# Adding the outputs of a mixture of experts by one-hot products instead of scattered rows, with experts grouped in triples

## The chip, the cores and the metric

The kernel runs on one core of one Trainium2 chip. The metric is the device time of one execution in microseconds. TensorE is called PE in the rows (PEld is its weight load), VectorE is DVE, ScalarE is ACT, GpSimd is POOL and the engine that issues most DMAs is SP. Everything is computed in 32-bit floats.

## The reference, cut to what matters

The reference is one layer of a decoder: two attention branches, then a mixture of experts. 320 tokens (256 of a prompt, 64 of eight samples) go through it. Only the second part is touched by the change:

```python
x = x + g1[:, None, :] * ((m_a * o_a + m_b * o_b) @ lw['w_out'])
h2 = modulate(rms_norm(x, lw['norm_ffn_g']), sh2, sc2)
x = x + g2[:, None, :] * hmoe(h2, lw['w_router_grp'], lw['w_router_exp'], lw['w_expert_in'], lw['w_expert_out'])
...
# in hmoe: each token takes one group of 4, and in it the best two of 8 experts
hid = jnp.einsum('nd,edf->nef', t, w_ein)
a, b = jnp.split(hid, 2, axis=-1)
act = jax.nn.silu(a) * b * combine[..., None].astype(hid.dtype)
return jnp.einsum('nef,efd->nd', act, w_eout)
```

There are 32 experts. Each has 1024 x 512 weights in and 256 x 1024 weights out, which is 3.15 MB. Every token goes to two experts, so there are 640 rows of 1024 values to compute and to add up by token. At the end comes a last RMSNorm over the 320 tokens.

## The kernel before, in words

Ahead of the experts the kernel projects the input (L565, L628, L672), runs both kinds of attention (L747 to L1013), the branch and the output projection (L1022, L1038), and routes on VectorE (L1990 to L2190). POOL fills the DRAM tensor `y_rows` (2 x 320 rows of 4 KB) with zeros early on (L2279), among other writes.

The normed rows are stored to DRAM (`h_rows`). Each expert gets slots in a *pair* of 128 slots. There are 16 pairs. Pairs 0 to 2 hold the fixed experts 0 to 5 with 64 slots each. The other 26 experts are sorted by the number of their rows on the chip, and pair `p` from 3 on takes rank `p - 3` (96 slots) and rank `28 - p` (32 slots). Rows beyond an expert's room would go into extra pairs, which run only if there are any.

What happens for pair `p`, with the engine and the line:

- POOL gathers the 128 rows out of `h_rows` (`gather`, L2348). This waits until the buffer of pair `p - 3` has been turned.
- PE turns them (`turn_rows`, L1117), ACT and DVE copy the result out of PSUM (L1497, L2035).
- PE multiplies with the weights in (`hidden`, L1159: 64 products of 32 slots by 512 columns, in two halves of 32, since the weights come in two halves too).
- ACT applies Silu (L1488), DVE multiplies (L2039), PE turns (`turn_act`, L1175), DVE copies (L2043).
- PE multiplies with the weights out (`pair_output`, L1186: 32 products), ACT and DVE scale the two halves by the routing weight into a row buffer `yeS` (L1508, L2049).
- POOL scatters the rows to `y_rows` (`scatter`, L2355).

PE runs `hidden(p)`, `turn_rows(p + 1)`, `pair_output(p - 1)`, `turn_act(p)` in this order. SP issues the weight loads in the order of use. Three pairs fit into SBUF, so that the weights in of pair `p` are asked for when `hidden(p - 3)` is done (L485), and the weights out when `pair_output(p - 3)` is done (L504):

```python
sp.wait_ge(s_hd, p - 2)
...
sp.wait_ge(s_od, 2 * (p - 2))
```

The rows of the last two pairs, 14 and 15, are not scattered. For these the kernel builds a one-hot matrix of 128 slots by 320 tokens on DVE (L2197), and PE multiplies a chunk of 128 channels of the row buffer with it (`early_hits`, L1143; L1245 in the tail): that gives the rows by token and turned. DVE then adds it, gated, to the residual `xT`, in three instructions for each of 8 chunks (`residual`, L1951, L1952, L1954).

The tail comes last: POOL waits for all scatters and signals (L2385), SP loads `y_rows` back in 12 pieces (L542), DVE adds the two rows of each token (L2233), PE turns them (L1240) and adds the product for pair 15 (L1245), DVE adds to the residual, ACT squares (L1544), PE sums (L1248), DVE takes the root's reciprocal (L1573) and scales (L2251), and SP stores the output (L546).

## Time and profile before

| What | Value |
|---|---|
| Median of 3 runs | 753.32 us (751.76 to 755.59) |
| The profiled execution | 755.45 us |
| Its span in the profile | 753.8 us |
| PE busy | 696.9 us (92% of the span) |
| DVE, ACT, POOL busy | 278.3, 172.0, 84.5 us |
| Bytes moved by DMA | 236.15 MB, mean 313 GB/s |
| Weights in, first pair of the sorted experts asked for | at 508 us |

A row of the timeline gives the start, the duration, the engine, the line and the operation with output and input, how many instructions it merges, and in brackets how long the engine had been idle before it and what ended that. The page divides the span into 40 equal slices; each is 18.8 us. "DMA arena<-in_w_ein" as the end of a wait means that a load of weights in landed.

### The profile page before, as it was taken

The page shows a single profiled execution, that of the slowest core. Times are in us where ns is not written, and L with a number is a line of the kernel's source. Part 1 is how long each engine was busy: PE and PEld are TensorE (multiplying, and loading weights), DVE is VectorE, ACT ScalarE, POOL GpSimd, SP SyncE. Part 2 cuts the span into 40 slices and gives each one's busy share as a digit, 9 for nine tenths or more (in the row PEclk, how much of TensorE's full clock was granted, in tenths as well). Part 3 has the DMA queues.
Part 4 walks back from the last instruction along what each step waited for, and adds up shares of the span by engine and source line. Part 5 has one row for each costly group of instructions (what it writes and reads, how often), then busy time and mean ns, then how long its engine had stood idle before and what let it go on. Part 6 is the DMA issues. An engine that isn't in the chain of part 4 may idle for free.

```text
span 753.8 us, 13479 instructions
## 1 busy us (share of the span) xinstructions
PE 696.9 (92%) x5136; PEld 398.8 (53%) x5136; DVE 278.3 (37%) x886; ACT 172.0 (23%) x410; POOL 84.5 (11%) x127
## 2 busy tenths in 40 slices
PE   5899899999999999799998999999999997888894
PEld 2687577558776665454555776664333332222342
DVE  2553123610102787664530322485411211111256
ACT  0223344112102564322242001331110101010102
POOL 0201000002500343110000000001212121112000
PEclk9999999999999999999999999999999999999998
DMA  8999997717344963899999992438999999999981
GB/s 239 383 411 396 410 366 236 309 68 276 113 157 180 359 256 120 313 363 389 392 378 385 420 407 87 191 104 312 419 418 418 418 419 417 419 419 418 420 254 72
DMA packets 63273, 236.15 MB, mean 313 GB/s; under 512 B 9733, under 2 KB 20878, under 8 KB 48293
## 3 DMA queue, kind: packets, MB, share of 16 engines
q1 hardware_dynamic: 52884, 218.73, 74.9%
q0 software_dynamic: 6432, 14.74, 5.3%
q10 hardware_dynamic: 3888, 1.77, 0.9%
q8 instruction: 43, 0.70, 0.4%
q14 instruction: 26, 0.20, 0.1%
HBM read 230.52 MB, written 19.14 MB: 331 GB/s over the span
## 4 chain that ended last, share of the span: by engine, by line
PE 62%; DMA 16%; SPq 13%; DVE 4%; issue 3%; ACTq 1%; ACT 1%; POOL 0%; POOLq 0%; DVEq 0%
PE bank L628 12%; SPq L485 7%; PE bank L1159 5%; PE bank L1038 5%; PE bank L1022 5%; SPq L504 4%; DMA arena<-in_w_eout 4%; DMA arena<-in_w_in 4%; PE bank L672 3%; PE bank L747 2%; PE bank L1186 2%; PE bank L565 2%; PE bank L970 2%; DMA arena<-h_rows,rows_of_slots_in 2%; PE bank L884 2%
## 5 line engine op out<-in xcount | busy, mean ns | idle before, releaser
L1159 PE MATMUL bank<-arena 128*32 128x512 f32 (+1 forms) x896 | 110.9, 610 | 14.2 <-DMA arena<-in_w_ein 14.0
L628 PE MATMUL bank<-arena 128*128 128x320 f32 x384 | 107.6, 439 | 2.8 <-DMA arena<-in_w_in 2.8
L628 PEld LDWEIGHTS bank<-arena 128*128 128x128 f32 x384 | 72.9, 191 | 34.7 <-DMA arena<-in_w_in 3.1
L1159 PEld LDWEIGHTS bank<-arena 128*32 128x32 f32 (+1 forms) x896 | 31.2, 114 | 82.9 <-issue 77.6
L1186 PE MATMUL bank<-arena 128*32 128x512 f32 (+1 forms) x464 | 58.3, 595 | 4.5 <-DMA arena<-in_w_eout 4.1
L2035 DVE COPY arena<-bank 128x512 f32<-128x512 f32 x14 | 9.7, 692 | 108.0 <-PE bank L1117 108.0
L1488 ACT ACTIVATE arena<-bank 128x256 f32<-128x256 f32 x16 | 6.2, 386 | 149.9 <-PE bank L1159 146.9
L1312 ACT ACTIVATE arena<-bank 32x320 f32<-32x320 f32 x60 | 25.8, 430 | 45.5 <-PE bank L628 45.0
L1038 PE MATMUL bank<-arena 128*128 128x320 f32 x128 | 35.0, 432 | 0.0
L1022 PE MATMUL bank<-arena 128*128 128x320 f32 x128 | 34.8, 432 | 0.0
L1186 PEld LDWEIGHTS bank<-arena 128*32 128x32 f32 (+1 forms) x464 | 15.6, 112 | 36.2 <-issue 29.8
L2355 POOL DMA_INDIRECT y_rows<-arena,rows_of_slots_out x14 | 14.1, 1010 | 151.0 <-DVE arena L2049 135.9
L1038 PEld LDWEIGHTS bank<-arena 128*128 128x128 f32 x128 | 24.1, 189 | 10.2
L1022 PEld LDWEIGHTS bank<-arena 128*128 128x128 f32 x128 | 24.1, 189 | 10.3
L1672 DVE TENSOR_TENSOR arena<-arena 128x320 f32<-128x320 f32 x15 | 7.4, 493 | 54.7 <-ACT arena L1313 54.7
L2049 DVE TENSOR_SCALAR arena<-bank,arena 128x512 f32<-128x512 f32 x15 | 11.3, 751 | 44.1 <-PE bank L1186 44.1
L565 PE MATMUL bank<-arena 128*32 128x128 f32 x768 | 23.7, 273 | 0.2 <-DMA arena<-in_w_ada 0.2
L565 PEld LDWEIGHTS bank<-arena 128*32 128x32 f32 x768 | 20.6, 108 | 4.5 <-issue 4.2
L1951 DVE SCALAR_TENSOR_TENSOR arena<-bank,arena 128x256 f32<-128x256 f32 x24 | 11.6, 483 | 28.0 <-PE bank L1038 24.2
L1357 ACT ACTIVATE arena<-arena 128x128 f32<-128x128 f32 (+1 forms) x48 | 21.1, 444 | 2.6 <-DVE arena L1746 2.6
L672 PE MATMUL bank<-arena 128*128 128x512 f32 (+1 forms) x64 | 21.6, 496 | 0.0
L580 PE MATMUL bank<-arena 128*128 128x256 f32 x64 | 16.5, 411 | 4.5 <-DMA arena<-in_cmp_pages 4.5
(413 smaller groups left out, 1011.5 us busy)
## 6 DMA issues: line engine op xcount, KB each, us to landing
arena<-in_w_ein SPq DMA_DIRECT2D x52, 1024.0 KB, 25.2
arena<-in_w_eout SPq DMA_DIRECT2D x26, 1024.0 KB, 26.9
arena<-in_w_ada SPq DMA_DIRECT2D x12, 2048.0 KB, 14.3
arena<-in_w_in SPq DMA_DIRECT2D x10, 2048.0 KB, 10.4
arena<-in_k_pages SPq DMA_DIRECT2D x64, 320.0 KB, 6.0
arena<-in_v_pages SPq DMA_DIRECT2D x64, 320.0 KB, 9.2
arena<-in_w_ein SPq DMA_DIRECT2D x3, 4096.0 KB, 21.8
arena<-in_w_eout SPq DMA_DIRECT2D x3, 2048.0 KB, 13.1
```

Of the source, the lines that this page charges most:

```text
L485: sp.dma_start(wi2[p % 3][:, u, 4 * part:4 * part + 4].rearrange("p k n -> p (k n)"), w_ein[bass.ds(of[u], 1), :, 2048 * part:2048 * part ...
L504: sp.dma_start(wo2[p % 3][:, u].rearrange("p k n -> p (k n)"), w_eout[bass.ds(of[u], 1), :, :].rearrange("o p n -> (o p) n")).then_inc(s_w ...
L565: m = mm(banks[6 + n % 2][32 * j:32 * (j + 1), 0:P].rearrange("p (c d) -> p c d", d=32), condS[:, k, :], columns[:, j], start=(k == 0), st ...
L580: m = mm(banks[2 * v][:, 0:256].rearrange("p (g j m) -> p g j m", g=2, m=4), w1s[v][:, t, :], odd, start=(t == 0), stop=(t == 7))
L628: m = mm(banks[c % 4][:, 0:N], ring[q][:, k, P * (c % 4):P * (c % 4 + 1)], hT[:, k, :], start=(k == 0), stop=(k == KD - 1))
L672: m = mm(bank[0:tn, 0:width], hT[:, k, t0:t0 + tn], ring[q][:, k, 0:width], start=(k == 0), stop=(k == KD - 1))
L1022: m = mm(banks[2 * (c % 2) + a][:, 0:N], wbr_sb[:, 4 * a + k, P * c:P * (c + 1)], src[:, k, :], start=(k == 0), stop=(k == 3))
L1038: m = mm(banks[4 + c % 2][:, 0:N], wo_sb[:, k, P * c:P * (c + 1)], mT[:, k, :], start=(k == 0), stop=(k == KD - 1))
L1159: m = mm(banks[2 + p % 2][r:r + n, :], xeT[p % 2][:, k, r:r + n], wi2[p % 3][:, e, k, :], start=(k == 0), stop=(k == KD - 1))
L1186: m = mm(banks[6 + half][r:r + n, :], actT[:, p % 2, j, r:r + n], wo2[p % 3][:, e, j, 512 * half:512 * (half + 1)], start=(j == 0), stop=( ...
L1312: act(qr[32 * r:32 * (r + 1), c % 3, :], banks[c % 4][32 * (r ^ 1):32 * (r ^ 1) + 32, 0:N], ACT.Copy)
L1357: m = act(seg, seg, ACT.Exp, bias=st[:, 4 + j:5 + j], scale=SCALE, accum_out=st[:, 8 + j:9 + j])
```

## The change

The rows of a unit of work are no longer scattered to DRAM. The kernel multiplies each unit's row buffer with a one-hot matrix, as it did for the last two pairs, and DVE adds the result to the residual chunk by chunk. `y_rows`, its zeros, the scatters, the loads at the end, the sums and the turning in the tail are gone.

There are 12 *units* in place of 16 pairs: the three fixed pairs, one sorted pair (ranks 0 and 25; 96 and 32 slots), and eight triples. Unit `p` from 4 on takes the ranks `p - 3` (64 slots), `p + 5` and `28 - p` (32 slots each). SBUF still holds six experts. Even units use places 2, 3, 4 and odd units 5, 0, 1, so that a triple's weights are asked for when the unit two before it has used that place.

The one-hot products come in halves of four chunks, `by_token(q, half)`. Three tables lay down where PE and DVE do them for an earlier unit `q` while working on unit `p`: before `hidden(p)`, between its halves, and behind it. PE now computes `hidden(p)`, `turn_act(p)`, `turn_rows(p + 1)` and the output of unit `p` itself, in that order, where before the output was that of pair `p - 1`. PSUM banks 0, 1, 3 and 5 take the products, so `hidden` uses bank 2 alone, `turn_act` bank 4 alone, and `turn_rows` waits until two residual chunks have freed banks 0 and 1. The one-hot matrix of a unit is one DVE instruction (`hits_of`). For the last unit the weights out are loaded in two halves by column.

```diff
+UNITS = 12
+LAST = UNITS - 1
+MIDDLE, LIGHT = 9, 17
+BEFORE = {4: (0, 0), 5: (1, 0), 6: (2, 0), 7: (3, 1), 8: (5, 0), 9: (6, 1), 10: (8, 0), 11: (9, 1)}
+AMID = {6: (2, 1), 7: (4, 0), 8: (5, 1), 9: (7, 0), 10: (8, 1), 11: (10, 0)}
+BEHIND = {4: (0, 1), 5: (1, 1), 6: (3, 0), 7: (4, 1), 8: (6, 0), 9: (7, 1), 10: (9, 0), 11: (10, 1)}
...
+            def places_of(p):
+                if p < 4 or p >= UNITS:
+                    return (0, 1) if p >= 3 else (2 * p, 2 * p + 1)
+                return (5, 0, 1) if p % 2 else (2, 3, 4)
...
@@ sync
+            sp.wait_ge(s_hd, 2)
+            unit_in(4, fourth, (0, 1))
+            sp.wait_ge(s_od, 2)
+            unit_out(3, third, (0, 1))
+            sp.wait_ge(s_hd, 3)
+            unit_in(4, fourth, (2,))
+            unit_in(5, fifth, (0,))
...
+            for p in range(6, UNITS):
+                of = experts_of(p)
+                sp.wait_ge(s_hd, p - 1)
+                unit_in(p, of, (0, 1, 2))
+                sp.wait_ge(s_od, 2 * (p - 1))
+                if p < LAST:
+                    unit_out(p, of, (0, 1, 2))
...
-            sp.wait_ge(s_ya, 1)
-            for half in range(2):
-                part = slice(512 * half, 512 * (half + 1))
-                for t, (t0, tn) in enumerate(TOK):
-                    for r in range(2):
-                        sp.dma_start(yR[0:tn, t, r, part], y_rows[N * r + t0:N * r + t0 + tn, part])\
-                            .then_inc(s_yl[3 * half + t], 16)
@@ tensor
+            def by_token(p, half):
+                te.wait_ge(s_hm, p + 1)
+                te.wait_ge(s_yD if half else s_yA, p + 1)
+                for c in range(4 * half, 4 * half + 4):
+                    if 8 * p + c >= 4:
+                        te.wait_ge(s_x2, 8 * p + c - 3)
+                    mm(four_banks[c % 4][:, 0:N], yeS[p % 4][:, P * c:P * (c + 1)], hits[p % 2], start=True, stop=True).then_inc(s_yt, 1)
...
+            for p in range(4, LAST):
+                hidden(p)
+                turn_act(p)
+                turn_rows(p + 1)
+                for half in range(2):
+                    unit_output(p, half)
...
+            with te.If(n_extra < 1):
+                unit_output(LAST, 0)
+                last_by_token(0)
+                unit_output(LAST, 1)
+                last_by_token(1)
+                square_sums()
@@ vector
+            for p in range(4, UNITS):
+                by_token(*BEFORE[p])
+                if p in AMID:
+                    by_token(*AMID[p])
+                pair_act(p)
+                if p < LAST:
+                    by_token(*BEHIND[p], 0, 2)
+                    act_out(p)
+                    by_token(*BEHIND[p], 2, 4)
+                    rows_out(p + 1)
+                    pair_out(p)
+                else:
+                    act_out(p)
+                    by_token(*BEHIND[p])
@@ gpsimd
-            po.dma_start(y_rows.rearrange("(t p) d -> p t d", p=P),
-                         zeros.unsqueeze(1).to_broadcast([P, 2 * N // P, D])).then_inc(s_zf, 16)
...
-            def scatter(p):
-                po.wait_ge(s_yA, p + 1)
-                po.wait_ge(s_yD, p + 1)
-                po.indirect_dma_start(out=y_rows, out_offset=bass.IndirectOffsetOnAxis(row_out[:, p:p + 1], 0),
```

The weights out are stored on the host by column half first. The arithmetic on VectorE that gives each row its slot is changed to fit the units; it has as many steps as before, within a few.

## Rows read from the trace of the kernel before

**Rows 1.** The page, 40 equal slices: bytes moved by DMA in each.
```profile
GB/s 239 383 411 396 410 366 236 309 68 276 113 157 180 359 256 120 313 363 389 392 378 385 420 407 87 191 104 312 419 418 418 418 419 417 419 419 418 420 254 72
```

**Rows 2.** Busy time by stretch: PE, PEld, DVE, ACT, POOL, PEclk, DMA share, GB/s.
```profile
80.00:85.00 5.00, 4.00 (x9) 2.60 (x10) 0.38 (x2) 0.00 (x0) 0.00 (x0) 0.66 1.03 407
508.00:528.00 20.00, 18.94 (x110) 9.50 (x111) 10.27 (x41) 3.24 (x7) 3.32 (x4) 1.00 0.82 303
528.00:718.00 190.00, 171.12 (x1388) 57.02 (x1388) 38.06 (x99) 23.06 (x41) 28.01 (x29) 0.98 1.02 418
718.00:734.00 16.00, 14.58 (x105) 6.28 (x98) 7.34 (x19) 1.76 (x3) 0.00 (x0) 1.00 0.84 249
```

**Rows 3.** Timeline of PE, one pair at full pace, then a wait: start, us, instruction.
```profile
602.36 7.07 PE L1159 MATMUL bank<-arena 128*32 128x512 f32 x64
609.37 1.09 PE L1117 MATMUL bank<-arena 128*128 128x128 f32 x8
610.39 3.64 PE L1186 MATMUL bank<-arena 128*32 128x512 f32 x32
613.96 0.44 PE L1175 MATMUL bank<-arena 128*128 128x128 f32 x2
...
619.17 3.64 PE L1159 MATMUL bank<-arena 128*32 128x512 f32 x32 [1.20 <-DMA arena<-in_w_ein]
```

**Rows 4.** The page, DMA issues: weights of the sorted experts, time from issue to landing.
```profile
arena<-in_w_ein SPq DMA_DIRECT2D x52, 1024.0 KB, 25.2
arena<-in_w_eout SPq DMA_DIRECT2D x26, 1024.0 KB, 26.9
```

**Rows 5.** DMA queues between 528 and 718 us: packets, MB, share of 16 engines.
```profile
q1 hardware_dynamic: 10265, 74.77, 94.5%
q0 software_dynamic: 3888, 4.52, 6.7%
```

**Rows 6.** Timeline of PE and POOL around the early wait.
```profile
59.30 0.90 POOL L2279 DMA_DIRECT2D y_rows<-arena  x1 [0.15 <-issue]
...
76.19 1.98 PE L565 MATMUL bank<-arena 128*32 128x128 f32 x64
81.00 19.23 PE L628 MATMUL bank<-arena 128*128 128x320 f32 x64 [2.83 <-DMA arena<-in_w_in]
...
102.06 17.54 PE L628 MATMUL bank<-arena 128*128 128x320 f32 x64
```

**Rows 7.** DMA between 54 and 81 us: POOL's queue, and two of its issues.
```profile
q0 software_dynamic: 347, 5.09, 48.5%
...
out_win_new<-in_win_state POOLq DMA_DIRECT2D x2, 2016.0 KB, 15.6
y_rows<-arena POOLq DMA_DIRECT2D x1, 2560.0 KB, 29.0
```

**Rows 8.** Timeline of the last two pairs and of the end: start, us, instruction.
```profile
709.65 3.64 PE L1186 MATMUL bank<-arena 128*32 128x512 f32 x32 [0.94 <-DMA arena<-in_w_eout]
713.22 2.42 PE L1143 MATMUL bank<-arena 128*128 128x320 f32 x8
...
714.06 0.48 DVE L1951 SCALAR_TENSOR_TENSOR arena<-bank,arena 128x256 f32<-128x256 f32 x1
...
715.05 0.48 DVE L1951 SCALAR_TENSOR_TENSOR arena<-bank,arena 128x256 f32<-128x256 f32 x1
...
724.66 0.39 ACT L1488 ACTIVATE arena<-bank 128x256 f32<-128x256 f32 x1 [12.33 <-PE bank L1159]
...
726.03 0.42 DVE L2043 COPY arena<-bank 128x256 f32<-128x256 f32 x1 [0.53 <-PE bank L1175]
...
742.51 0.23 DVE L1954 TENSOR_TENSOR arena<-arena 128x64 f32<-128x64 f32 x1
```

**Rows 9.** Timeline of PE: the same 32 products behind two waits.
```profile
651.68 5.22 PE L1159 MATMUL bank<-arena 128*32 128x512 f32 x32 [2.26 <-DMA arena<-in_w_ein]
...
683.76 3.64 PE L1159 MATMUL bank<-arena 128*32 128x512 f32 x32 [1.42 <-DMA arena<-in_w_ein]
```

More of the change, by code:

```diff
@@ L482, in _, with experts_of, half_in @@
                 sp.dma_start(h_rows[RT * t:RT * (t + 1), :], hR[t][0:RT, :]).then_inc(s_hst, 16)
-            def half_in(p, part, of, s):
-                for u in range(2):
-                    sp.dma_start(wi2[p % 3][:, u, 4 * part:4 * part + 4].rearrange("p k n -> p (k n)"),
+            def experts_of(p):
+                ranks = (0, FREE_E - 1) if p == 3 else (p - 3, p + 5, 28 - p)
+                return [sp.value_load(order[0:1, r:r + 1], min_val=0, max_val=E - 1) for r in ranks]
+            def half_in(p, of, part, which):
+                s = s_wh[p % 3] if part else s_wi[p % 3]
+                for u in which:
+                    sp.dma_start(in_of(places_of(p)[u])[:, 4 * part:4 * part + 4].rearrange("p k n -> p (k n)"),
@@ L507, in _ @@
             sp.wait_ge(s_ord, 1)
-            this = sorted_pair(3)
-            after = sorted_pair(4)
-            sorted_in(3, this)
-            for p in range(3, LAST - 1):
-                sorted_in(p + 1, after)
-                sorted_out(p, this)
-                this, after = after, sorted_pair(p + 2)
-            sorted_out(LAST - 1, this)
-            sorted_in(LAST, after)
-            sorted_out(LAST, after)
+            third = experts_of(3)
+            sp.wait_ge(s_hh, 2)
+            half_in(3, third, 0, (0, 1))
@@ L1199, in _ @@
             turn_rows(1, (1,))
-            for p in range(1, LAST):
+            for p in range(1, 4):
                 hidden(p)
@@ L1246, in tail, with square_sums @@
+            def square_sums():
                 for k in range(KD):
@@ L1515, in _ @@
             rows_out(0)
-            for p in range(LAST):
+            for p in range(4):
                 if p:
@@ L1525, in _ @@
                     pair_out(p - 1)
-            pair_out(LAST - 1)
+            pair_out(3)
+            for p in range(4, LAST):
+                pair_silu(p)
+                rows_out(p + 1)
+                pair_out(p)
             pair_silu(LAST)
@@ L1946, in _, with residual @@
             ve.wait_ge(s_x, 32)
-            def residual(c, bank, g0, s, before=0):
+            def residual(c, bank, g0, s, before=0, gated=None):
                 if before + c:
@@ L2222, in extra_pair @@
                 pair_out(p)
+                for c in range(KD):
+                    ve.wait_ge(s_yx, 8 * x + c + 1)
+                    residual(c, banks[5], 40, s_xr, 8 * x, s_xg)
+                ve.wait_ge(s_xr, 8 * (x + 1))
                 if x + 1 < EXTRA // 2:
@@ L2227, in tail @@
             def tail():
-                def row_sums(half, t):
-                    tn, part = TOK[t][1], slice(512 * half, 512 * (half + 1))
-                    ve.wait_ge(s_yl[3 * half + t], yl_before[3 * half + t] + 32)
-                    ve.tensor_tensor(yR[0:tn, t, 0, part], yR[0:tn, t, 0, part], yR[0:tn, t, 1, part], ALU.add).then_inc(s_ysum, 1)
-                def last_residual(first, last):
-                    for c in range(first, last):
-                        ve.wait_ge(s_yt, KD + c + 1)
-                        residual(c, banks[c], 40, s_x2, KD)
-                for t in range(3):
-                    row_sums(0, t)
-                row_sums(1, 0)
-                row_sums(1, 1)
-                last_residual(0, 1)
-                row_sums(1, 2)
-                last_residual(1, KD)
+                for c in range(KD):
+                    ve.wait_ge(s_yt, 8 * LAST + c + 1)
+                    residual(c, banks[LAST_BANKS[c]], 40, s_x2, 8 * LAST)
                 ve.wait_ge(s_ss3, 1)
@@ L2365, in _ @@
             po.wait_ge(s_rows, 3)
-            for p in range(LAST - 1):
-                if p + 3 < PAIRS:
-                    gather(p + 3)
-                scatter(p)
+            for p in range(3, UNITS):
+                gather(p)
             po.wait_ge(s_ord, 2)
@@ L2382, in _ @@
             extra_pair(0)
-            for k in range(3):
-                po.wait_ge(s_ys[k], 16 * ((LAST + 1 - k) // 3))
-            po.memset(cst[:, C_SIN:C_SIN + 1], 0.0).then_inc(s_ya, 1)
 def cond_rows():
```

403 lines of the change are left out of this document (217 added, 186 removed).

## The prediction

> **What bounds the kernel now.** I read the page first and the expert stage after it. The slices of the page show where DMA is full: from the 29th on, ten slices in a row move 417 to 420 GB/s [rows 1]. The windows say the same: 418 GB/s and every DMA engine busy from 528 to 718 us, with PE busy 171 of these 190 us [rows 2]. Which of the two sets the pace shows in the timeline of PE. One pair at full pace takes 7.07 + 1.09 + 3.64 + 0.44, about 12.0 us from one `hidden` to the next [rows 3]. Up to 614 us PE runs at this pace and lives on what was loaded ahead. Then it waits for weights in each pair. An expert is 3.15 MB, so a pair is 6.3 MB, or 15.0 us at 418 GB/s. DMA is the slower of the two. The stage ends when the stream of 26 sorted experts (81.8 MB) ends, plus a tail. The loads of weights take 25 to 27 us to land because they stand in line [rows 4].
>
> When does that stream end? Between 718 and 734 us 16 x 249 GB/s = 4.0 MB arrive [rows 2], and 2.62 MB of them are the 640 rows of 4 KB read back. So 1.36 MB of weights were still to come at 718 us; without the read-back they would be in at 718 + 3.3 = **721.3 us**. From there to 753.8 us is a tail of 32 us, of which the trip through DRAM (last scatter, signal, read-back) takes the most.
>
> I work in times of the profiled execution (755.45 us, span 753.8) and carry the difference over to the median, 753.3 us.
>
> **The scatters.** They go, and with them the bytes in the full stream. By the reference's routing, counted on its inputs drawn with seed 0, pairs 3 to 15 hold 510 rows (gathered after 528 us) and pairs 0 to 13 hold 590 (scattered). Together that is 1100 x 4 KB = 4.51 MB; the trace has 4.52 MB on POOL's queue [rows 5], so the count fits. The scatters' part is 590/1100. By bytes: 2.42 MB / 418 GB/s = 5.8 us. By the queue's share of the engines: 6.7% of 190 us = 12.7 us, times 590/1100 = 6.8 us. I take 6.3 us between them. It counts in full, since the stream is full. The gathers stay: the same rows in fewer, fuller units.
>
> **The zeros.** `y_rows` is filled at 59.30 us, 2.62 MB, and lands 29.0 us later [rows 6, 7]. In its time PE waits 2.83 us for a tile of `w_in` [rows 6]. On POOL's queue 5.09 MB had moved by 81 us; 4.13 MB are the two window copies and 0.13 MB another zero tile, so 0.83 MB of the zeros stood before that tile [rows 7]. Without them it lands 0.83 MB / 395 GB/s = 2.1 us sooner, and 0.7 us of the wait is left. After the wait the granted clock is 0.66 of full over 80 to 85 us [rows 2], that is part of it at the lower level of 1.2 GHz, and the next 64 products take 19.23 us where the same take 17.54 later [rows 6]. A wait under 1.5 us costs no such dip [rows 9], so 1.7 us more are saved. PE is the bound from there to the expert stage, so everything shifts by 2.1 + 1.7 = 3.8 us. Ends: 0 (other loads take the place) and 4.5 us (the whole wait and the dip). The Trainium skill, "DMA: Bandwidth & Descriptors", section "Queues, rings and completion order", says that each DMA engine takes turns between queue rows, packet by packet. By that rule the zeros take up to an equal turn while they are in flight, and the gain would stand near its upper end, the median at 736.0 us. POOL's queue had about half of the engine time there [rows 7], which agrees.
>
> **Triples in place of pairs.** A unit of PE is the 12.24 us of 7.07 + 1.09 + 3.64 + 0.44 [rows 3] and eight one-hot products, 2.42 us [rows 8]: 14.66 us. Its 9.44 MB take 22.6 us. So PE has 7.9 us to spare per unit, and 12 units instead of 16 even lower its sum. DVE adds 8 residual chunks at 0.99 us (start to start, [rows 8]) to some 2.3 us of copies: about 10.5 of 22.6 us, hidden. What falls away as cover is the room in SBUF: triples wait for the unit two before. Does the stream run dry? The tightest moment is the end of `hidden(4)`, which asks for unit 6. At 12.0 us per pair `hidden(3)` starts at 542.5 us; output 3 and the first one-hot products now stand before `hidden(4)`, which ends about 567. Weights asked for by then: units 3 to 5, eight experts, 25.2 MB. Landed: about 6 MB by 528 [rows 2, 5], and 39 us at 405 GB/s (74.8 MB of SP's queue and 2.4 MB in the scatters' place, over 190 us), together 21.7 MB. 3.5 MB or 8 us are left, so it does not run dry. From unit 8 on the end of a `hidden` leaves 11 MB in line, the 25 to 27 us in line seen before [rows 4]. Cost: nothing; if PE were over 8 us late at unit 4 each further us would be lost whole. Shorter waits of SP, POOL and the changed slot arithmetic (a few instructions under 0.3 us) are hidden by the same stream.
>
> **The tail.** Stream end: 721.3 - 6.3 - 3.8 = 711.2 us. The last unit's weights out (3.15 MB, 7.5 us) come behind its weights in, which would land at 703.7. Loads smear, though: at 709.65 us PE gets the weights out of pair 14 [rows 8] with 6.29 MB still behind them, which by bytes should end at 724.7 and not 721.3. I add that 3.4 us: 707.1. Then the second half of `hidden(11)`. It takes 3.64 us, or 5.22 behind a wait of 2.26 us [rows 9]; waits between the pieces will be 2 to 3 us, so I take 5.2: 712.3. Silu, product, turning and copy: 1.9 us from the products' end (724.59) to 726.45 [rows 8]: 714.2. Now DVE is the bound. It still has four residual chunks of unit 10 and eight of unit 11, 12 x 0.99 = 11.9 us: 726.1. PE fits in between: its half outputs (1.8 us), ACT's copy (0.7 us) and a product of 0.3 us are ready 0.6 us before DVE wants the second half. From the last residual at 742.74 to the span's end are 11.1 us of squares, root, scaling and store [rows 8], unchanged: **737.2 us**. That is 16.6 us less, of which 3.8 are early, 6.3 the scatters, 6.5 the tail. The median goes to 753.3 - 16.6 = 736.7 us.
>
> On the clock the skill speaks against the change. "TensorE: Matmul & The Clock Gate", section "HAM oscillation — how this bites in real kernels", says that a loop whose compute is shorter than its wait for data starts each tile at half rate. Taken for the whole piece that is 7.3 us for the last half of `hidden` and 738.8 us in all. The row shows less: 5.22 us instead of 3.64, so the higher level came back inside the piece, and the sum goes by it.
>
> **The rivals.**
> *Slower: TensorE stays at its lower level.* It idles 35% of a triple. If all its products ran at 1.2 GHz, a unit would take 29.3 us against 22.6, eight units 54 us more: about 790 us. It decides from 22.6/14.66 = 1.54 times the work on, and the kernel is slower than before from 1.68 times. For it: the two dips above. Against it: clock 0.98 over the stage [rows 2], and each dip ended inside its piece. 4%. The page just named, taken as a rule for every tile, would lead here.
> *The stream has holes.* If triples ask too late at units 4 to 7, or the smear leaves DMA engines idle, some 5 to 10 us are lost: 742 to 747 us. The 8 us margin speaks against it. 15%.
> *The early gain stays out*, as the window copies hold the tile: 736.7 + 3.8 = 740.5. 15%.
> *The tail is shorter*: no smear, no dip, 5.0 us less, 731.7. 12%.
> *It does not do what it says*: extra units would run if an expert overflowed. The sorted counts are 67, then 44 to 24 for ranks 1 to 8, then at most 19, against room for 96, 64 and 32. None runs. Another 3% for a change of no effect by some cause that I don't see.
>
> **How the numbers follow.** My forecast has 51% and its own range is 733 to 740. Low end of the whole: scatters 6.8, early 4.5, no smear and no dip, 730.5, and a little for faster DMA: 729. High end: the second rival's 746. Outside are the first rival and some edges, under 2 in 10. A measurement of this kernel can tell about 0.5%, 3.8 us, from no change. All cases but the first and the last lie below 749.5: faster 0.93, same 0.03, slower 0.04.
>
> **What would show it right or wrong.** Right: no wait at the `w_in` tile, or one under 1 us; 418 GB/s without a hole until about 711 us; waits of PE for both weights in every unit from 6 on; twelve residual chunks in a row on DVE before the squares. Wrong: slices under 410 GB/s in the stage, PEclk below 0.9 there, DVE waiting for products in the tail.

## The result, and the profile after

The changed kernel takes **748.11 us** (median of 20 runs, 741.89 to 752.78); the kernel before took 754.86 us on the same chip (20 runs, 750.94 to 758.18). The ratio is **0.9915**, 95% interval 0.9894 to 0.9935. So it is faster, but by 6.7 us instead of 16.6. A ratio of 0.001 is 0.75 us throughout. The profiled execution took 749.36 us, with a span of 747.7 us.

The slices of DMA, columns as in [rows 1], with the clock of PE above them:

```profile
PEclk9999999999999999999999999998999999999987
GB/s 254 388 417 395 383 264 235 316 48 278 114 156 183 356 265 114 315 353 383 392 392 386 418 425 104 197 116 227 361 418 419 420 419 420 420 421 419 419 142 73
```

The stream has no hole from the 30th slice on, as forecast. But it starts no earlier than before: slices 28 and 29 have 227 and 361 GB/s against 312 and 419 in [rows 1], and above the 28th the clock shows an 8. The queues of 524 to 714 us (packets, MB, share of 16 engines):

```profile
q1 hardware_dynamic: 10772, 76.48, 97.5%
q0 software_dynamic: 1296, 2.09, 3.0%
```

The same stretch by busy time, columns as in [rows 2]:

```profile
524.00:714.00 190.00, 174.60 (x1176) 73.18 (x1178) 99.81 (x336) 17.41 (x31) 10.01 (x10) 0.99 1.01 415
```

The scatters' bytes are gone from POOL's queue (4.52 MB in [rows 5]) and SP's queue has 1.7 MB more in the same 190 us. PE is busy 174.6 us of them, more than before in [rows 2], although there are fewer hidden products. The timeline of PE over one unit shows why (start, us, instruction; L1189 and L1221 are the hidden and output products, L1169 the one-hot ones):

```profile
681.56 3.64 PE L1189 MATMUL bank<-arena 128*32 128x512 f32 x32 [1.47 <-DMA arena<-in_w_ein]
685.13 2.42 PE L1169 MATMUL bank<-arena 128*128 128x320 f32 x8
689.00 3.64 PE L1189 MATMUL bank<-arena 128*32 128x512 f32 x32 [1.45 <-DMA arena<-in_w_ein]
692.57 2.42 PE L1169 MATMUL bank<-arena 128*128 128x320 f32 x8
694.83 0.38 PE L1208 MATMUL bank<-arena 128*128 128x128 f32 x2
695.46 1.06 PE L1148 MATMUL bank<-arena 128*128 128x128 f32 x8 [0.25 <-DVE arena L2032]
696.45 3.64 PE L1221 MATMUL bank<-arena 128*32 128x512 f32 x32
700.02 2.42 PE L1169 MATMUL bank<-arena 128*128 128x320 f32 x8
703.91 3.64 PE L1189 MATMUL bank<-arena 128*32 128x512 f32 x32 [1.47 <-DMA arena<-in_w_ein]
```

From 681.56 to 703.91 is one unit, 22.35 us. Between the others stand three lines of 2.42 us, and there are only two waits of note, 2.9 us together. The kernel issues four products (`by_token`, one half of a unit's chunks) where the row says x8: each such product leaves two records in the trace. The forecast took a group of eight records for all eight products.

**Where the gain went.** At 475 us the changed kernel's profile is 4.55 us ahead: the router's first product (L1071, before L1043) starts at 475.23 against 479.78. Of this lead 1.86 us were there at the products on the next tile of `w_in` (100.20 against 102.06 in [rows 6]). The rest came later, in work that the change leaves as it was, and single profiles differ there by as much (see the zeros below). All of the lead, and more, is lost at one place. Here are PE, POOL and SP around 502 us, first after, then before:

```profile
501.60 3.84 PE L1117 MATMUL bank<-arena 80*128 80x128 f32 x32
502.27 1.15 POOL L2426 DMA_INDIRECT arena<-h_rows,rows_of_slots_in  x1 [25.96 <-DVE rows_of_slots_in L2200]
502.32 24.06 SPq L504 DMA_DIRECT2D arena<-in_w_ein  x8
510.82 1.11 PE L1148 MATMUL bank<-arena 128*128 128x128 f32 x4 [5.38 <-DMA arena<-h_rows,rows_of_slots_in]
511.87 4.67 PE L1199 MATMUL bank<-arena 128*64 128x512 f32 x16
517.05 5.37 PE L1189 MATMUL bank<-arena 128*64 128x512 f32 x24
```

```profile
506.82 1.15 POOL L2348 DMA_INDIRECT arena<-h_rows,rows_of_slots_in  x1 [25.96 <-DVE rows_of_slots_in L2123]
507.96 16.76 SPq L485 DMA_DIRECT2D arena<-in_w_ein  x8
```

POOL issues the gather of unit 1's rows, and SP the first in-weights of unit 3 (two loads of 1 MB). Before, SP issued 1.14 us behind POOL; after, 0.05 us. The gather then takes 8.5 us to landing instead of 3.8, PE waits 5.38 us for it where it waited 0.7, and the hidden products behind it run in part at the low clock (4.67 us for the 16 records that take 3.65; the granted clock is 0.50 from 511 to 513 us). The hidden products of unit 1 start at 517.05, and started at 515.42 before: a lead of 4.55 us has become a lag of 1.63. The cause stands in SP's program. Before, SP read four expert numbers (of pairs 3 and 4) ahead of these loads; after, it reads only unit 3's two, and unit 4's behind the loads. SP's loads started 1.50 us behind the end of the DVE instruction that releases the reads (L2195, 500.82 us), and 2.59 us behind it before (L2118, 505.37). The two reads are this difference of 1.09 us, some 0.55 us each. That was the theory for the runs below.

**The tail**, from the last in-weights on (PE, and DVE's first residual piece and last one):

```profile
712.93 6.50 PE L1189 MATMUL bank<-arena 128*32 128x512 f32 x32 [3.02 <-DMA arena<-in_w_ein]
719.37 2.42 PE L1169 MATMUL bank<-arena 128*128 128x320 f32 x8
721.62 0.38 PE L1208 MATMUL bank<-arena 128*128 128x128 f32 x2
...
722.38 0.48 DVE L2024 SCALAR_TENSOR_TENSOR arena<-bank,arena 128x256 f32<-128x256 f32 x1
...
727.05 0.48 DVE L2024 SCALAR_TENSOR_TENSOR arena<-bank,arena 128x256 f32<-128x256 f32 x1 [0.86 <-PE bank L1266]
...
734.80 0.23 DVE L2032 TENSOR_TENSOR arena<-arena 128x64 f32<-128x64 f32 x1
```

The last in-weights land at 712.93 us (forecast 707.1), the hidden half takes 6.50 us (forecast 5.2), and one group of one-hot products stands ahead of the turning. DVE's twelve residual chunks run from 722.38 to 735.03 us, in 12.65 us.

### The profile page after: what moved, and what is told of

Its sections match the earlier page's. It is cut to its first block, busy times and chain, and to the rows that moved or that the text cites. A ratio compares the mean times of both kernels' runs of the same rounds, so it can differ in the third digit from the quotient of the medians.

```text
span 747.7 us, 13116 instructions
## 1 busy us (share of the span) xinstructions
PE 693.2 (93%) x4848; PEld 409.4 (55%) x4848; DVE 334.8 (45%) x1111; ACT 164.8 (22%) x398; POOL 64.3 (9%) x106
## 3 DMA queue, kind: packets, MB, share of 16 engines
q10 hardware_dynamic: 3888, 1.77, 0.9%
## 4 chain that ended last, share of the span: by engine, by line
PE 66%; DMA 15%; SPq 11%; DVE 3%; issue 2%; ACTq 1%; ACT 1%; POOL 0%; POOLq 0%; DVEq 0%
PE bank L656 12%; SPq L504 6%; PE bank L1189 6%; PE bank L1066 5%; PE bank L1050 5%; DMA arena<-in_w_ein 4%; DMA arena<-in_w_in 4%; PE bank L1221 3%; PE bank L700 3%; DMA arena<-in_w_eout 3%; PE bank L775 2%; SPq L514 2%; PE bank L593 2%; PE bank L998 2%; PE bank L912 2%
## 5 line engine op out<-in xcount | busy, mean ns | idle before, releaser
L656 PE MATMUL bank<-arena 128*128 128x320 f32 x384 | 107.6, 439 | 2.2 <-DMA arena<-in_w_in 2.2
L1189 PE MATMUL bank<-arena 128*32 128x512 f32 (+1 forms) x640 | 81.9, 614 | 10.8 <-DMA arena<-in_w_ein 10.8
L656 PEld LDWEIGHTS bank<-arena 128*128 128x128 f32 x384 | 72.8, 191 | 34.1 <-DMA arena<-in_w_in 2.5
L2024 DVE SCALAR_TENSOR_TENSOR arena<-bank,arena 128x256 f32<-128x256 f32 x104 | 50.2, 483 | 48.6 <-PE bank L1066 24.2
L1189 PEld LDWEIGHTS bank<-arena 128*32 128x32 f32 (+1 forms) x640 | 22.0, 115 | 62.2 <-issue 47.8
L1169 PE MATMUL bank<-arena 128*128 128x320 f32 x176 | 53.3, 444 | 0.0
L1221 PE MATMUL bank<-arena 128*32 128x512 f32 (+1 forms) x336 | 45.6, 618 | 3.4 <-DMA arena<-in_w_eout 2.0
L1169 PEld LDWEIGHTS bank<-arena 128*128 128x128 f32 x176 | 31.5, 188 | 29.3 <-issue 18.7
L1554 ACT ACTIVATE arena<-bank 128x256 f32<-128x256 f32 x12 | 4.6, 385 | 139.8 <-PE bank L1189 135.8
L1066 PE MATMUL bank<-arena 128*128 128x320 f32 x128 | 35.0, 432 | 0.0
L1050 PE MATMUL bank<-arena 128*128 128x320 f32 x128 | 34.8, 432 | 0.0
L1066 PEld LDWEIGHTS bank<-arena 128*128 128x128 f32 x128 | 24.1, 189 | 10.2
L1050 PEld LDWEIGHTS bank<-arena 128*128 128x128 f32 x128 | 24.1, 189 | 10.3
L1221 PEld LDWEIGHTS bank<-arena 128*32 128x32 f32 (+1 forms) x336 | 12.1, 116 | 27.9 <-issue 25.0
L2032 DVE TENSOR_TENSOR arena<-arena 128x64 f32<-128x64 f32 x104 | 23.5, 226 | 3.5
L2025 DVE TENSOR_TENSOR arena<-bank,arena 128x64 f32<-128x64 f32 x104 | 22.3, 215 | 0.0
L2426 POOL DMA_INDIRECT arena<-h_rows,rows_of_slots_in x11 | 11.3, 1029 | 123.5 <-PE bank L1148 95.4
## 6 DMA issues: line engine op xcount, KB each, us to landing
arena<-in_w_eout SPq DMA_DIRECT2D x3, 2048.0 KB, 15.4
```

What stands on the lines that cost most here:

```text
L656: m = mm(banks[c % 4][:, 0:N], ring[q][:, k, P * (c % 4):P * (c % 4 + 1)], hT[:, k, :], start=(k == 0), stop=(k == KD - 1))
L1050: m = mm(banks[2 * (c % 2) + a][:, 0:N], wbr_sb[:, 4 * a + k, P * c:P * (c + 1)], src[:, k, :], start=(k == 0), stop=(k == 3))
L1066: m = mm(banks[4 + c % 2][:, 0:N], wo_sb[:, k, P * c:P * (c + 1)], mT[:, k, :], start=(k == 0), stop=(k == KD - 1))
L1169: mm(four_banks[c % 4][:, 0:N], yeS[p % 4][:, P * c:P * (c + 1)], hits[p % 2], start=True, stop=True).then_inc(s_yt, 1)
L1189: m = mm(banks[3 if p == 1 else 2][r:r + n, :], xeT[p % 2][:, k, r:r + n], in_of(places_of(p)[e])[:, k, :], start=(k == 0), stop=(k == KD ...
L1221: m = mm(banks[6 + half][r:r + n, :], actT[:, p % 2, j, r:r + n], out_of(places_of(p)[e])[:, half, j, :], start=(j == 0), stop=(j == 1))
```

## The experiments

Ratios are to the kernel before, measured on the same chip in the same session. The runs are called e1 to e12 by the heads of their names.

**Reading earlier (e1).** SP reads unit 4's numbers ahead of the loads again, which puts 1.7 us between the gather and the loads and changes nothing else.

```diff
             third = experts_of(3)
+            fourth = experts_of(4)
             sp.wait_ge(s_hh, 2)
             half_in(3, third, 0, (0, 1))
-            fourth = experts_of(4)
```

> The changed kernel, with SP reading the expert numbers of unit 4 before it issues the first loads of unit 3, as the kernel before did: these loads start some 1.7 us later (three reads at 0.56 us). Theory 'the gather was overtaken': in the changed kernel the 2 MB of loads start at 502.32 us, 0.05 us behind the gather's issue, and get to the DMA engines ahead of its rows; the gather takes 8.5 us instead of 3.8 and TensorE waits 5.38 us. Then here the gather lands after about 4 us, the wait falls under 1 us, the slow products behind it go back to full pace, and the time falls by 5 to 6.5 us from 748.1, to about 742 (ratio to before about 0.984). Rival 'DMA bounds the stage anyway': the wait is shorter, but the stream ends when it did, and the time stays at 748 (0.991), or even rises by the 1.7 us.

Measured: 742.18 us, ratio **0.985** (0.9829 to 0.9872). POOL, SP and PE in its timeline:

```profile
505.53 1.15 POOL L2426 DMA_INDIRECT arena<-h_rows,rows_of_slots_in  x1 [25.96 <-DVE rows_of_slots_in L2200]
507.23 16.15 SPq L504 DMA_DIRECT2D arena<-in_w_ein  x8
509.17 0.66 PE L1148 MATMUL bank<-arena 128*128 128x128 f32 x4 [0.47 <-DMA arena<-h_rows,rows_of_slots_in]
```

The wait is 0.47 us instead of 5.38. One line of SP's program is worth 0.0065, or 4.9 us, give or take 2.2 (both intervals together).

**Waiting for the gather (e2).** The same is reached in another way: SP waits for the landing, with the numbers still read late.

```diff
+            sp.wait_ge(s_xl[1], 16)
             half_in(3, third, 0, (0, 1))
```

> The changed kernel, with SP waiting until the gather of unit 1 has landed before it issues the first loads of unit 3. Theory 'the gather was overtaken': the gather takes 3.8 us, TensorE waits under 0.7 us there, and the time is about 742, at most 1 us from that of the kernel that reads first. Rival 'the loads' start sets the end': the stream of weights starts about 4 us later than in the changed kernel, and the time is 748 to 752.

Measured: 741.72 us, ratio **0.9853** (0.9837 to 0.987). Its timeline:

```profile
506.48 0.66 PE L1149 MATMUL bank<-arena 128*128 128x128 f32 x4 [0.33 <-DMA arena<-h_rows,rows_of_slots_in]
...
706.81 3.64 PE L1190 MATMUL bank<-arena 128*32 128x512 f32 x32 [3.01 <-DMA arena<-in_w_ein]
```

Here SP's loads go out 3.7 us after the gather (502.97 and 506.65 us), and it costs nothing that can be told from zero against the run before: what counts is the order, not the time of the loads. The last in-weights land at 706.81 us, 6.1 us earlier than in the changed kernel's profile.

**The same order in the kernel before (e4, e9, e10).** If the theory is right, the kernel before must lose as much when its loads come early. SP issues them ahead of the reading of pair 4's numbers.

```diff
             this = sorted_pair(3)
+            sp.wait_ge(s_hh, 2)
+            half_in(3, 0, this, s_wi[0])
             after = sorted_pair(4)
-            sorted_in(3, this)
+            sp.wait_ge(s_hd, 1)
+            half_in(3, 1, this, s_wh[0])
```

> The kernel before, with the first loads of pair 3 issued ahead of the reading of pair 4's expert numbers: 1.1 us earlier, at about the gather's own issue. Theory 'the gather was overtaken': the same stall appears here, the gather lands after 8 us or more, TensorE waits about 5 us, and the time rises by 3 to 6 us over before (ratio 1.004 to 1.008). Rival 'only the units matter': no change, ratio within 0.002 of 1.

Measured: 760.62 us, ratio **1.0106** (1.009 to 1.0122). That is 8.0 us more, beyond the 3 to 6 that were expected, and the profile did not show the mechanism: a low clock at 504 to 511 us held PE and with it SP, the loads went out at 511.99 us, 2.9 us behind the gather, and the gather landed in 3.6 us. This execution was slow in other ways: it waited 4.88 us for the tile of `w_in`, started the router 2.2 us later than the kernel before, and took 6.58 us for the products below that take 3.65.

```profile
505.21 6.58 PE L1170 MATMUL bank<-arena 128*64 128x512 f32 x16
511.73 3.84 PE L1092 MATMUL bank<-arena 80*128 80x128 f32 x32
515.40 0.60 PE L1120 MATMUL bank<-arena 128*128 128x128 f32 x4
```

So the same kernel was profiled once more.

> The same kernel as e4_before_early_load (the kernel before with the in-loads of unit 3 issued ahead of the reading of pair 4's two numbers), once more for a second profile, since the first took 760.6 us in the median but showed a low clock at 503 to 511 us, which held SP back, instead of a gather that was overtaken. Theory (the loads go out with the gather, 1.1 us earlier against it, and overtake it): the gather takes over 7 us to landing, PE waits 4 to 6 us for its rows and has a low clock behind; 758 to 762 us. Rival (the low clock around 505 us comes of this order and is the whole loss): gather at 3.6 us, low clock again.

Measured: 763.69 us in its one execution, beside 754.58 us. Its timeline now has the whole pattern of the changed kernel:

```profile
507.44 1.15 POOL L2351 DMA_INDIRECT arena<-h_rows,rows_of_slots_in  x1 [25.96 <-DVE rows_of_slots_in L2126]
507.49 16.73 SPq L485 DMA_DIRECT2D arena<-in_w_ein  x4
515.93 1.12 PE L1120 MATMUL bank<-arena 128*128 128x128 f32 x4 [5.32 <-DMA arena<-h_rows,rows_of_slots_in]
516.98 6.19 PE L1170 MATMUL bank<-arena 128*64 128x512 f32 x16
```

0.05 us between the issues, 8.4 us to landing, a wait of 5.32 us, and slow products behind it. They are slower here than in the changed kernel (6.19 us, not 4.67), so that the hidden products of unit 1 start at 523.69 us, 7.7 us later against the gather's issue than before (16.25 us behind it, not 8.60). The control keeps the early order and adds the wait for the gather:

```diff
+            sp.wait_ge(s_xl[1], 16)
             half_in(3, 0, this, s_wi[0])
```

> e4_before_early_load with SP made to wait for the landing of unit 1's gather ahead of the in-loads of unit 3: the early order of SP, but nothing that can overtake. Theory (e4's 7 us are the overtaken gather): as the kernel before, or up to 2 us slower since the loads leave some 2 us later than there: ratio 1.000 to 1.003. Rival (e4's loss has another cause in SP's order or the clock): ratio 1.008 to 1.011 again.

Measured: 755.05 us against 754.58, ratio **1.0007** (0.9985 to 1.0028). The loss is gone with the collision: 0.0099 of ratio, 7.5 us, give or take 2, between e4 and e10. In the kernel before the order costs more than the 4.7 to 4.9 us of the changed kernel; the slower products of e9 would account for 1.5 us of that, but they stand in one profile. Both kernels lose by the early loads and recover when the gather goes first, so this cause is shown; its size in the kernel before rests on the times and one profile.

**The scatters' price (e6).** All rows of the scatters are sent out of bounds in the kernel before.

```diff
-            ve.tensor_copy(row_out[:, :], to)
+            ve.tensor_scalar(row_out[:, :], to, 0.0, NOWHERE, ALU.mult, ALU.add)
```

> The kernel before with the target rows of every scatter set out of bounds, so that the nine scatters move no rows (left out: the writing of the expert rows, so y lacks the experts added through them). Theory of the prediction (the weight stream is what bounds the stage and the scatters' 2.4 MB took 5.8 to 6.8 us of it): 6.3 us less than before, ratio 0.9917. Rival (scattered rows went in the queue's gaps beside the stream): 0 to 1 us less, ratio 0.999 to 1.000. Rival (the scatters' small rows disturb the stream by more than their bytes): 8 to 12 us less, ratio 0.986.

Measured: 749.08 us, ratio **0.9945** (0.9924 to 0.9966), that is 4.1 us less, with 2.6 to 5.7 in the interval. Its queues between 528 and 718 us:

```profile
q1 hardware_dynamic: 11078, 76.18, 97.6%
q0 software_dynamic: 3888, 2.10, 3.8%
```

2.42 MB left the queue, exactly the forecast's count. By bytes they are 5.8 us, which is just outside the interval. But the packets stayed: q0 has 3888 in both kernels. 14 scatters (the expectation said nine) and 13 gathers share them, 144 each, as the nine gathers of the changed kernel have 1296. And the queue takes 3.8% of the engines here against 3.0% there for the same bytes. So scatters without rows still cost something, by that difference up to 1.5 us (an estimate, 0.8% of 190 us), and the price of 4.1 us may be that much too low. Neither the bytes nor the share (6.8 us) is ruled out as the better guide.

**The read-back's bytes (e11).** Of each 512 columns read back at the end of the kernel before only 64 are read; seven eighths of the read-back is left out.

```diff
-  sp.dma_start(yR[0:tn, t, r, part], y_rows[N * r + t0:N * r + t0 + tn, part])
+  sp.dma_start(yR[0:tn, t, r, part.start:part.start + 64],
+               y_rows[N * r + t0:N * r + t0 + tn, part.start:part.start + 64])
```

> The kernel before with 64 of each 512 columns of the expert rows read back at the end (left out: seven eighths of the read-back, 2.3 of its 2.62 MB, so y is made from what the buffer held there). It prices the read-back's bytes apart from the trip's fixed delay. Theory of the prediction (the read-back stands beside the last weights, which end 3.4 us earlier without it, and behind the last scatter): 4 to 6 us less, ratio 0.992 to 0.995. Rival (the last scatter, its signal and the fixed delay of a load make the trip, bytes are nothing): 0 to 1.5 us less. Rival (bytes are most of the tail): 8 us less or more.

Measured: 753.16 us, ratio **0.9988** (0.9967 to 1.001). The bytes were worth 0.9 us, nothing that can be told from zero: the theory misses and its rival holds. In the timelines the last pair takes as long with the bytes as without: from the outputs of pair 14 to the turning of pair 15 it is 15.91 us in both (709.65 to 725.56 before, 708.73 to 724.64 here). Only the turning of the read rows is 1.0 us shorter (8.28 and 7.29 us from its first transpose to the square sums). The 2.3 MB moved beside work that was there anyway. The last weights out landed at 726.1 us before (issued at 696.8, 29.3 us to landing) and at 723.9 here (695.8, 28.1 us). The outputs of pair 15, which need them, started at 726.56 and 725.64 us, each 0.1 us behind DVE's copy of the turned activations, which they need too (DVE L2043, ended 726.45 and 725.54). So the last pair was held by the chain of PE and DVE, and weights that land earlier win nothing there.

**The zeros' price (e3, e7).** The 2.62 MB are written again, once in the changed kernel and once in the kernel with the gather first. The only edit is the fill at its old place and its buffer (`y_rows`).

```diff
+            po.dma_start(y_rows.rearrange("(t p) d -> p t d", p=P),
+                         zeros.unsqueeze(1).to_broadcast([P, 2 * N // P, D])).then_inc(s_zf, 16)
```

> The changed kernel with the 2.62 MB of zeros written to a DRAM tensor again, at the place where the kernel before wrote them; nothing reads them. The prediction's term: 3.8 us slower than the changed kernel, 752 (ratio to before 0.996), with a wait of 2.8 us at the tile of w_in. Rival 'the window copies hold the tile': the changed kernel still waits 2.22 us there, so the zeros are worth 0.6 us of the wait and no clock dip, and the time is 748.1 to 749 (0.991 to 0.992).

> e2_gather_first with the 2.62 MB of zeros written as before, so that their price is read without the late gather. Theory of the prediction: 3.8 us more than e2_gather_first (2.1 of the wait for the tile of w_in and 1.7 of TensorE's low clock behind it), ratio 0.990. Rival (e3_zeros_back against the changed kernel, 0.0033 of ratio, is the whole price): 2 to 3 us more, ratio 0.9885. Rival (the wait has causes of its own and the zeros cost nothing): within 1 us of e2_gather_first.

Measured: e3 748.62 us, ratio 0.9948 (0.9929 to 0.9967), against 0.9915 without the fill; e7 741.9 us, ratio 0.9858 (0.9816 to 0.9899), against 0.9853. So the zeros cost 2.5 us by the first pair and 0.4 by the second, with some 2 and 3 us of uncertainty. The rows of the wait for the tile of `w_in` show how much it varies. First the changed kernel, then e2 and e7:

```profile
79.14 19.23 PE L656 MATMUL bank<-arena 128*128 128x320 f32 x64 [2.22 <-DMA arena<-in_w_in]
```

```profile
79.20 17.54 PE L657 MATMUL bank<-arena 128*128 128x320 f32 x64 [1.90 <-DMA arena<-in_w_in]
```

```profile
80.20 19.22 PE L657 MATMUL bank<-arena 128*128 128x320 f32 x64 [2.70 <-DMA arena<-in_w_in]
```

In e3's own profile, with the zeros, the wait is only 0.80 us and the products behind it take 17.54 us. One execution says little here, so I took the same row from all 14 profiles of the study (its 64 records are 32 products):

| kernels | profiles | wait, us | mean | products behind it slow | router starts, us, mean |
|---|---|---|---|---|---|
| with the zeros (before, e3, e4, e6, e7, e9, e10, e11) | 8 | 0.80 to 4.88 | 2.81 | 7 of 8 | 476.2 to 482.0, 479.2 |
| without (after, e1, e2, e5, e8, e12) | 6 | 0.77 to 2.71 | 1.76 | 2 of 6 | 475.2 to 479.5, 477.1 |

The wait is 1.0 us shorter in the mean, and the slow products (1.4 to 1.7 us) come in 2 of 6 instead of 7 of 8, which is another 0.9 us. The start of the router, at which all these kernels have done the same work but for the zeros, is 2.1 us earlier (with a spread of 1.8 us between profiles, so the difference is uncertain by 2 us). The wait and the slow products are where the forecast had them, and all this points to **about 2 us** rather than 3.8; but each number alone leaves room for anything from about 0 to 4.

**The products' price, and TensorE's room (e8).** Four of the one-hot products of each unit are done twice in the kernel with the gather first: 2.42 us more in each of eight units.

```diff
+                    if twice:
+                        mm(four_banks[c % 4][:, 0:N], yeS[p % 4][:, P * c:P * (c + 1)], hits[p % 2], start=True, stop=True)
```

> e2_gather_first with the four one-hot products ahead of each unit's hidden products done twice, 2.42 us more of TensorE in each of units 4 to 11 (19.4 us in all; the result is the same). Theory (the trace after the change: the stream sets the pace of 22.35 us a unit, TensorE has 2.9 us to spare in it from unit 8 on, and ahead of that it works off a delay without letting the stream run dry): 2.4 us more from the last unit at most and 0 to 2 from the earlier ones, 742 to 746 us, with the waits for in-weights of 1.45 us shrunk to a few tenths. Rival of the prediction (7.9 us to spare in a unit): 0 to 2.4 us more and still some 5 us of waits in a unit. Rival (TensorE is as tight as the stream, and what it does later frees buffers later): 10 to 19 us more, 752 to 761 us, with holes in the stream.

Measured: 743.63 us, ratio **0.9876** (0.9844 to 0.9908): 0.0023, or 1.7 us, for 19.4 us more of PE's work. The stretch of 600 to 700 us in e2 and in this kernel, columns as in [rows 2]:

```profile
600.00:700.00 100.00, 91.07 (x630) 39.25 (x626) 60.29 (x202) 8.36 (x15) 2.02 (x2) 1.00 1.01 420
```

```profile
600.00:700.00 100.00, 98.76 (x654) 44.94 (x646) 58.22 (x194) 8.35 (x15) 2.03 (x2) 1.00 1.01 420
```

DMA moves 420 GB/s in both. PE goes from 91 to 99 us of 100, and no wait for in-weights is left among the waits of this stretch. So the one-hot products are hidden, as forecast, but the room that hides them was 2.9 us a unit, and this run uses nearly all of it.

**A shorter tail (e5).** The one-hot products and residuals of unit 10's second half move from behind the last hidden products into the wait between their halves.

```diff
-BEHIND = {..., 10: (9, 0), 11: (10, 1)}
+BEHIND = {..., 10: (9, 0)}
...
                         if p in AMID:
                             by_token(*AMID[p])
+                        if p == LAST:
+                            by_token(LAST - 1, 1)
```

> The changed kernel with the gather ahead of SP's loads (as e2_gather_first, ratio 0.985), and besides the four products and residuals of unit 10's second half, which stood behind the last unit's hidden products, put between the halves of those products, where TensorE waited 3.01 us for the last in-weights in that profile. Theory (the tail is a chain: last hidden half, four one-hot products of 2.42 us, turning, twelve residuals of 0.99 us, square sums): the 2.42 us leave the chain and four residuals (4.0 us) move into the wait, while the last unit's own outputs become the limit; 3 to 4 us less than e2_gather_first, 738 us, ratio 0.980 to 0.981; the last unit's eight residuals then run without the other four ahead of them. Rival (the products and residuals move, but the in-weights' landing and the last outputs set the end, so only about 1 us comes off): 740.7 us. Rival (the wait ahead of the second half grows past the chip's patience and TensorE falls to its low clock for the rest of the tail): no gain or 1 to 3 us more.

Measured: 741.07 us, ratio 0.9843 (0.9809 to 0.9877), against 0.9853 for the same kernel without it: 0.7 us, with 2.8 us of uncertainty. The first rival's 740.7 us is near; the 3 us of the theory lie at the edge of the interval. The profiled execution was the slowest of the six (745.77 us) and had a low clock at 502 to 508 us, so only its tail is used here:

```profile
711.87 0.81 PE L1170 MATMUL bank<-arena 128*128 128x320 f32 x2 [0.17 <-DVE arena L2035]
712.85 0.81 PE L1170 MATMUL bank<-arena 128*128 128x320 f32 x2 [0.17 <-DVE arena L2035]
713.59 3.64 PE L1192 MATMUL bank<-arena 128*32 128x512 f32 x32
718.19 0.44 PE L1211 MATMUL bank<-arena 128*128 128x128 f32 x2 [0.96 <-DVE arena L2120]
719.19 1.92 PE L1224 MATMUL bank<-arena 128*32 128x512 f32 x16 [0.56 <-issue]
721.92 2.42 PE L1269 MATMUL bank<-arena 128*128 128x320 f32 x8 [0.80 <-ACT arena L1578]
724.27 1.93 PE L1224 MATMUL bank<-arena 128*32 128x512 f32 x16
727.00 2.42 PE L1269 MATMUL bank<-arena 128*128 128x320 f32 x8 [0.81 <-ACT arena L1581]
```

The wait of 3.01 us is filled. Of the short waits behind it 0.56, 0.80 and 0.81 stood in e2 as well; new is 0.96 us for DVE's activation product, which the group of 2.42 us had covered there. From the start of the last hidden half to the end of the square sums it is 20.1 us here (713.59 to 733.73) and 21.3 in e2 (706.81 to 728.12). So 1.2 us of the 2.42 leave the tail, since the products of the last unit itself, half by half, are a chain of their own.

**All three together (e12).** The early read, the wait for the gather, and the tail.

> The changed kernel with the three edits together: numbers of unit 4 read early (e1), SP's in-loads of unit 3 behind the landing of unit 1's gather (e2), and unit 10's second half between the halves of the last hidden products (e5). Theory (the gather's loss is 6 us and is gone by either of e1 and e2; e5's edit is worth 1.2 us by its profile, whose other time was a low clock that also comes without the edit): 740 to 741 us, ratio 0.983 to 0.985. Rival (early numbers gain on top): 739 us, 0.982. Rival (e5's edit is worth nothing): as e2_gather_first, 0.985 to 0.986.

Measured: **740.75 us**, ratio **0.9825** (0.9796 to 0.9854), the lowest of the study, though its interval overlaps those of e1, e2 and e5. The gather of unit 1 lands in 3.4 us, and the wait of 3 us in the last unit is filled as in e5:

```profile
708.26 0.81 PE L1170 MATMUL bank<-arena 128*128 128x320 f32 x2 [0.17 <-DVE arena L2035]
709.00 3.64 PE L1192 MATMUL bank<-arena 128*32 128x512 f32 x32
```

It beats the kernel before by 13 us and the changed kernel by 6.8, and most of the latter, 4.7 to 4.9 us by e1 and e2, is the order of one gather and two loads.

## Why the prediction was wrong

The sign was right and the mechanism of the stage too; the size was not. Forecast 0.978, measured 0.9915: 0.0135 or some 10 us are missing.

- **The step that failed** is the sentence "Shorter waits of SP, POOL and the changed slot arithmetic ... are hidden by the same stream". The diff shows SP's read of unit 4's numbers move behind the loads of unit 3. I took a shorter wait for a gain at worst hidden. What I did not ask is what SP's earlier issue runs into: the gather of unit 1, which PE needs at once, at a time when the stream is not yet full and PE sets the pace. Measured: 4.9 us (e1) and 4.7 us (e2), about half of what is missing. The rival "the stream has holes" had about the right size of loss (5 to 10 us) by the wrong cause: the stream has no hole, its full pace starts late.
- **The scatters**: 6.3 us forecast, 4.1 measured (e6), 2.2 us less. The count of bytes was right. Whether the price was wrong stays open: the interval ends at 5.7 us, and e6 may leave up to 1.5 us of the scatters in.
- **The zeros**: 3.8 us forecast, about 2 measured (0.4 and 2.5 in e7 and e3, 2.1 by the start of the router), so some 1.8 us too much. "0.7 us of the wait is left" failed: without the zeros 1.76 us are left in the mean, and the slow products behind the wait still come in a third of the profiles. The rival "the early gain stays out" (15%) holds half. By the turns between queue rows that the Trainium skill states ("DMA: Bandwidth & Descriptors", "Queues, rings and completion order") the forecast saw the gain near its upper end, 4.5 us. Some 2 us do not bear that out, though the interval of e3 (2.5 us, give or take 2.1) just reaches it.
- **The triples**: cost nothing, right in its result. The term was wrong twice: eight chunks are two groups of eight records, 4.84 us and not 2.42; and units 6 to 11 each do three groups, since `BEFORE`, `AMID` and `BEHIND` there catch up what the early units leave. With [rows 3] that is 12.24 + 3 x 2.42 = 19.5 us of PE in a unit, not 14.66, and the room is 2.9 us and not 7.9. e8 shows that even that was enough. The miscount is an older one: the description of the kernel before takes records for products too, so that its 64 products of `hidden` are 32 in the code and its 32 of `pair_output` are 16, and the forecast's "product of 0.3 us" in the tail is half a product. The times that it took from those rows stay right.
- **The tail**: in the changed kernel's own profile the landing came 5.8 us late, mostly the gather's debt. In e2's profile, without that debt, it came at 706.81 us against a forecast of 707.1. From there the forecast had 30.1 us to the end of the span, e2 31.5 (738.3 - 706.81, 1.4 us more), the changed kernel 34.8. The forecast took a hidden half with a dip (5.2 us) and got 3.64 in e2 and 6.50 in the changed kernel. It left out the one-hot group of 2.42 us ahead of the turning. That PE's outputs "are ready 0.6 us before DVE wants the second half" was a near miss: DVE waited 0.86 and 0.35 us, and the twelve chunks took 12.65 us instead of 11.9. From the last residual to the end were 12.7 us (735.03 to 747.7; 12.3 in e2) and not 11.1; 0.7 us of that is PE, which ends the square sums 2.07 us behind the last residual where it took 1.36 before.
- **The read-back** was taken for what holds the last weights in the kernel before, with the stream's end as the start of the tail. Leaving out seven eighths of it changed 0.9 us (e11): the last pair there was held by PE and DVE, not by the stream. What the tail gained is then the trip rather than its bytes; this is by subtraction, no run took the trip out by itself.
- **TensorE's clock**: 0.99 over 524 to 714 us. The first rival stayed out. PE was also idle far less than the 35% that it was given: 15.4 us of 190, or 8%.

Gather 4.8, scatters 2.2, zeros 1.8 and tail 1.4 make 10.2 us, against about 10 that are missing. The close agreement is luck: the terms are uncertain by 1.5 to 2 us each, and the tail's comes from one profile. That e2's last in-weights land within 0.3 us of the forecast is luck too, since scatters and zeros that gave 4 us less should have shown there. The two profiled executions alone, 740.05 over 755.45, make a ratio of 0.9796; the medians make 0.9853, 4 us more. Only the gather is far beyond its uncertainty and confirmed in both kernels. The 5.5 us that e2 is still missing are not settled term by term.

## What to carry to other kernels

When a change makes a queue's engine ready sooner, list what that queue issues next and which small, urgent transfer is in flight at that moment. Here two loads of 1 MB issued at the same instant as a gather delayed it by 4.7 us, and one semaphore wait, or a harmless instruction ahead of the loads, gave it back. Before pricing a wait by the bytes ahead of it, see how the same wait varies between executions; and count how many records one logical product leaves before a group's time is taken for a whole step.

## What the runs showed of the hardware

- A gather issued within 0.05 us of two 1 MB loads took 8.4 to 8.6 us to landing (after, e3, e9); issued 1.1 us or more ahead, 3.4 to 3.9 us (the other eleven profiles). The difference of some 4.8 us is about the time of 2.1 MB at 420 GB/s (5.0 us), as if the gather stood behind both loads. The taking of turns between queue rows that the Trainium skill states ("DMA: Bandwidth & Descriptors", "Queues, rings and completion order") would by itself cost a small gather less, so it does not explain these rows alone. Which part of the path makes the gather wait was not tried.
- Equal waits do not cost equal clock. Ahead of the last hidden half a wait of 3.01 us had no dip behind it (e2, 3.64 us), 3.07 us had one (4.95 us in e7), and 3.02 us a long one (6.50 us, after). At the tile of `w_in` five waits of 0.77 to 1.90 us had none, the nine of 2.22 us and more all did (18.98 to 19.23 instead of 17.54 us).
- In three profiles (e4, e5, e12) the granted clock fell to 0.50, the level of 1.2 GHz, for 3 to 7 us from 500 to 504 us on, although PE was busy throughout. Here is e5 (columns as in [rows 2]), with 1.00 ahead of it and behind:

```profile
501.00:503.00 2.00, 2.00 (x14) 1.87 (x15) 1.93 (x3) 0.00 (x0) 0.00 (x0) 0.70 0.03 8
503.00:505.00 2.00, 2.00 (x6) 0.48 (x4) 1.90 (x5) 0.00 (x0) 0.00 (x0) 0.50 0.00 0
```

It begins in or right behind eight products with 3 columns each (16 records) and costs 1.7 to 3 us (the next 16 records in 5.35 to 6.62 us instead of 3.65). The same instructions ran at full clock in the other eleven profiles; its cause stays open.
